# Values as the stationary operand in the second attention's two branches, with the probabilities scaled on VectorE before they are flipped

## What is computed

```
o_c = softmax(q kc^T) vc            # compressed keys, 31 of them
o_s = softmax(q ks^T, causal) vs    # selected blocks: with 512 tokens all of them are selected
o_w = softmax(q kw^T, causal) vw    # window of 512: the same reach
y_b = g_c * o_c + g_s * o_s + g_w * o_w
merged = gate_a * (y_a @ w_br_a) + gate_b * (y_b @ w_br_b)
```

## Time and profile before

| what | us |
|---|---|
| three runs, median (lowest to highest) | 1233.98 (1233.65 to 1234.14) |
| the profiled execution, its own time | 1236.62 |
| span of that execution, first to last instruction | 1234.8 |
| TensorE busy in it | 1197.2 (97%) |
| VectorE, GpSimd, ScalarE busy | 632.7, 676.4, 318.0 |
| the 64 steps, from the first score matmul to the last weigh matmul | 646.3 to 799.9 |
| first matmul on `yb_hi` | 803.9 |

### The profile page before, as it was taken

One profiled execution on the slowest core, in us unless ns is written; L12 is line 12 of the kernel. 1 busy time (PEld: TensorE's weight loads), 2 busy tenths in 40 slices (PEclk: granted clock), 3 DMA queues, 4 the chain that ended last, 5 costly groups with the idle time before them and its releaser, 6 DMA issues.

```text
span 1234.8 us, 18903 instructions
## 1 busy us (share of the span) xinstructions
PE 1197.2 (97%) x6856; PEld 985.0 (80%) x6856; DVE 632.7 (51%) x1212; ACT 318.0 (26%) x667; POOL 676.4 (55%) x610
## 2 busy tenths in 40 slices
PE   7999999998999999999999999999999999999997
PEld 6777778777987787877788888878888888888885
DVE  3885654478732576563876666572353300335022
ACT  3125112124632322211234454420221100113001
POOL 4884443343526587665743334356666666666662
PEclk9999999998799899999999999999999999999998
DMA  7221121114003222223531111122232332333321
GB/s 246 86 85 55 50 55 49 53 53 120 1 18 110 70 85 85 85 69 102 210 107 35 52 52 38 52 82 87 85 101 88 100 102 88 99 102 104 101 85 68
DMA packets 29684, 102.41 MB, mean 83 GB/s; under 512 B 3632, under 2 KB 6064, under 8 KB 28848
## 3 DMA queue, kind: packets, MB, share of 16 engines
q1 hardware_dynamic: 27232, 93.47, 24.1%
q10 hardware_dynamic: 2384, 7.99, 1.9%
HBM read 95.16 MB, written 2.10 MB: 79 GB/s over the span
## 4 chain that ended last, share of the span: by engine, by line
PE 85%; DVE 6%; POOL 4%; issue 2%; ACT 2%; DMA 1%; SPq 0%; DVEq 0%; POOLq 0%; ACTq 0%
PE acc L277 23%; PE acc L279 22%; PE acc L278 22%; POOL w_lo L1544 3%; PE aux L488 3%; PE aux L1600 2%; PE aux L478 2%; PE aux L344 1%; PE aux L1584 1%; PE aux L869 1%; PE acc L488 1%; PE aux L870 1%; DMA residual<-x 1%; PE aux L782 1%; DVE conv_sum L1911 1%
## 5 line engine op out<-in xcount | busy, mean ns | idle before, releaser
L1536 POOL CAST w_hi<-w_raw 128x1024 fp32r<-128x1024 f32 x164 | 177.7, 1083 | 504.2 <-issue 365.9
L1544 POOL TENSOR_TENSOR w_lo<-w_raw,w_hi 128x256 fp32r<-128x256 f32 x352 | 290.2, 855 | 7.0
L277 PE MATMUL acc<-ht_hi,w_hi 128*128 128x512 f32 x672 | 272.8, 406 | 6.3 <-DVE ht_lo L388 2.5
L279 PE MATMUL acc<-ht_hi,w_lo 128*128 128x512 f32 x672 | 264.2, 393 | 0.0
L278 PE MATMUL acc<-ht_lo,w_hi 128*128 128x512 f32 x672 | 263.7, 392 | 0.0
L1539 POOL TENSOR_TENSOR w_lo<-w_raw,w_hi 128x1024 fp32r<-128x1024 f32 x76 | 188.3, 2477 | 6.1
L277 PEld LDWEIGHTS acc<-ht_hi,w_hi 128*128 128x128 f32 x672 | 127.1, 189 | 37.2 <-POOL w_lo L1544 6.0
L279 PEld LDWEIGHTS acc<-ht_hi,w_lo 128*128 128x128 f32 x672 | 127.1, 189 | 27.6
L278 PEld LDWEIGHTS acc<-ht_lo,w_hi 128*128 128x128 f32 x672 | 127.4, 190 | 24.3 <-issue 1.2
L277 PE MATMUL acc<-w_hi,ht_hi 128*128 128x512 f32 x256 | 106.8, 417 | 0.3
L277 PE MATMUL acc<-w_hi,ff_hi 128*128 128x512 f32 x256 | 100.4, 392 | 2.3 <-POOL w_lo L1539 2.3
(11 more groups left out here) (413 smaller groups left out, 1949.4 us busy)
## 6 DMA issues: line engine op xcount, KB each, us to landing
w_raw<-units SPq DMA_DIRECT2D x164, 512.0 KB, 3.5
cmp_w<-w_kv ACTq DMA_DIRECT2D x4, 1024.0 KB, 7.8
residual<-x SPq DMA_DIRECT2D x4, 512.0 KB, 7.1
k_turned<-k_split SPq DMA_DIRECT2D x8, 256.0 KB, 5.0
result<-normalized SPq DMA_DIRECT2D x4, 512.0 KB, 2.6
consts_sb<-consts SPq DMA_DIRECT2D x1, 1120.5 KB, 7.3
k_turned<-k_split ACTq DMA_DIRECT2D x2, 512.0 KB, 5.9
norm_post_sb<-norm_post ACTq DMA_DIRECT2D x1, 512.0 KB, 4.2
```

The source lines that it names most:

```text
L277: nc.tensor.matmul(bank, ah, bh, start=start, stop=False)
L279: return nc.tensor.matmul(bank, al, bh, start=False, stop=stop)
L1536: nc.gpsimd.tensor_copy(w_hi[:, slot], raw[:, j]).then_inc(hi_split, 1)
L1544: done = nc.gpsimd.tensor_tensor(w_lo[:, slot, kk, cols], raw[:, j, kk, cols], w_hi[:, slot, kk, cols].bitcast(F32), ALU.subtract)
```

## The change

The values become the stationary operand (64 columns) and the flipped probabilities the moving one (128 columns). The two heads of a pair, both of one group, write to partitions 0 to 63 and 64 to 127 of the same bank, so that the result is features by tokens. The steps are reordered for that: n % 2 is the head of the pair, n % 8 // 2 the tile t. `weigh` runs once for a pair of steps, and in TensorE's order it stands ahead of `flip`. The reciprocal and the gate can no longer be applied to the result, where tokens lie along the columns; VectorE multiplies both onto the probabilities instead, between the exponential and the flip (`scale_probs`), and adds the result of a pair with `add_values`. `YB` becomes `YT`, features by tokens, so its flips at the end are gone, and the high and low parts of its chunks 0 to 2 are made within the steps. The compressed branch is written by feature too: 4 head pairs with 512 columns in place of 4 tiles with 2 x 256.

```diff
+            def flip(n):
+                branch, k, g, t, h = branch_step(n)
+                pe.wait_ge(values_used, SELECTED + n + 2)
+                if n:
+                    pe.wait_ge(probs_out, SELECTED + n)
+                for j in range(t + 1):
+                    done = nc.tensor.transpose(flips_to[:, j * P:(j + 1) * P], pr2[:, h, j * P:(j + 1) * P], ident)
+                done.then_inc(probs_flipped, 1)
+            def weigh(pair):
...
+                pe.wait_ge(probs_out, SELECTED + 2 * pair + 2)
+                pe.wait_ge(values_used, SELECTED + 2 * pair + 3)
...
+                for j in range(t + 1):
+                    for h in range(2):
+                        done = nc.tensor.matmul(values_to[h * DH:(h + 1) * DH, 0:P], VSW[:, j, a:a + DH],
+                                                pt2[:, h, j * P:(j + 1) * P], start=j == 0, stop=j == t)
+                done.then_inc(weighed, 1)
+            for n in range(BRANCH_STEPS):
+                scores(n + 1)
+                fill(n)
+                if n and n % 2 == 0:
+                    weigh(n // 2 - 1)
+                flip(n)
+            def scale_probs(n):
+                branch, k, g, t, h = branch_step(n)
+                w, m = (t + 1) * P, n % 16
+                eng.wait_ge(probs, SELECTED + n + 1)
+                step(nc.vector.reciprocal(rs8[:, m:m + 1], psum_[:, m:m + 1]))
+                nc.vector.tensor_scalar(pr2[:, h, :w], pr2[:, h, :w], rs8[:, m:m + 1], gate(branch, 2 * k + h, t),
+                                        ALU.mult, ALU.mult).then_inc(values_used, 1)
+            def add_values(pair):
+                y = YT[:, k, t * P:(t + 1) * P]
+                eng.wait_ge(weighed, SELECTED + pair + 1)
+                done = nc.vector.tensor_tensor(y, y, aux[3][:, 0:P], ALU.add)
+            for n in range(BRANCH_STEPS + 2):
+                if n < BRANCH_STEPS:
+                    negate(n)
+                    if 1 <= n % 8 < 5 and n < BRANCH_STEPS - 8:
+                        done = stage(n // 8 + 1, n % 8 - 1)
...
+                if 1 <= n <= BRANCH_STEPS:
+                    scale_probs(n - 1)
+                if n >= 3 and n % 2:
+                    add_values((n - 3) // 2)
+                beside(n)
...
+            def high_part(k):
+                act.wait_ge(on["y_summed"], k + 1)
+                nc.scalar.activation(yb_hi[:, k], YT[:, k], ACT.Copy).then_inc(flip_hi, 1)
...
+                if n in (46, 51, 59):
+                    high_part((n - 43) // 8 if n > 46 else 0)
...
-            for t in range(NT):
-                pe.wait_ge(on["c_flip_out"], t // 2 + 1)
+            pe.wait_ge(on["c_flip_out"], 2)
+            for k in range(4):
...
-            flip_on_tensor(pe, lambda t, k: YB[:, t, k * P:(k + 1) * P], 4, FLIP_B)
+            branches_on_tensor(pe, branch_fill)
```

## The result

| kernel | us, median (lowest to highest) | ratio to before | steps |
|---|---|---|---|
| before | 1233.83 (1233.65 to 1234.14), 4 runs | 1 | 153.8 |
| after | 1256.30 (1253.66 to 1258.51), 4 runs | 1.0174, 95% interval 1.0157 to 1.0191 | 178.6 |

The account below looks back on a forecast made before the run. TensorE was taken to bound the steps. -5.8 (weigh) + 27.5 (waits) - 4.0 (end) + 0.9 (compressed branch) = +18.6, with 1.4 for the clock +20: profiled 1236.6 becomes 1256.6, median 1254, range 1243 to 1270.

Parts of the forecast that it names:

- The weigh: TensorE's weigh matmuls in the steps: 25.1 us against 30.9, a gain of 5.8.
- whether the halves overlap: Weigh: rival that the two column halves don't overlap, 42.5 us in place of 25.1, time 1268; chance 0.05.
- The waits: TensorE's waits in the steps: 31.5 us with VectorE disturbed, 26.5 undisturbed; less 4 today, +27.5.
- the chain: Within a step: scores, negate, any stage, reciprocal, scaling on VectorE, then flip; fixed parts 0.74 us, covered by piece and weigh.
- The scaling's price: VectorE's scale_probs: 0.28, 0.35, 0.41, 0.48 us by width, taken from L1469.
- the rival built on it: Scaling at the price of L1190: 0.28 to 0.48 us more in waiting steps, time 1269; chance 0.06.
- The end: From the last weigh to the product on yb_hi: flips gone, early chunks already split, 4.0 us gained.
- The compressed branch: Its matmul waits for the second move; first score at 647.1, not 646.27: 0.9 us lost.
- The clock: Steps: a fall of the granted clock behind long waits; one costs at most 1.7 us, 1.4 added.
- the rival of some falls: Steps: waits bring on some falls of the clock, time 1261; chance 0.06.
- The rival of a clock that stays low: Steps: a stretch that stays at 1.2 GHz, time up to 1300; chance 0.03.
- The covered chain: Steps: VectorE's chain ends inside the piece, so only the savings are left, 1217; chance 0.07.

Follow-up runs that it names:

- e4: The changed kernel with the weigh's loops turned round, all key blocks for one head, then for the other: 1262.54 us, ratio to before 1.0230.
- e1: The changed kernel with scale_probs(n-1) put ahead of negate(n) and the staging of queries on VectorE: 1227.60 us, ratio to before 0.9948.
- e2: The changed kernel with only the staging of queries moved behind scale_probs(n-1), negate(n) still ahead: 1239.34 us, ratio to before 1.0043.
- e3: The changed kernel with scale_probs multiplying only the first column, the rest left unscaled: 1246.06 us, ratio to before 1.0096.
- e11: The changed kernel with the reciprocal of scale_probs made twice in each of 64 steps: 1264.35 us, ratio to before 1.0242.
- e5: The changed kernel with its nine steps without a piece moved to 2, 10, 18 to 58 and 63: 1257.41 us, ratio to before 1.0163.
- e7: The changed kernel with six useless 512-column matmuls added in each of the nine steps without a piece: 1258.47 us, ratio to before 1.0188.
- e6: e1 with the nine steps without a piece moved to 2, 10, 18 to 58 and 63: 1229.66 us, ratio to before 0.9954.
- e12: e1 with the reciprocal of scale_probs made twice in each step: 1233.85 us, ratio to before 0.9992.
- e8: e1 with the high and low parts of all four chunks of y_b put behind the 64 steps: 1233.40 us, ratio to before 0.9987.
- e10: e6 with step 6's output-gate piece made between the compressed branch's last matmul and the first score: 1229.67 us, ratio to before 0.9949.

## Why the prediction was right, step by step

**The weigh**, 25.1 us forecast. By the four widths measured (0.47, 0.69, 0.90 and 1.13 a pair with the way in) it is 25.5. The doubt whether the halves overlap as in the earlier trace rows is settled by these widths and by e4. The Trainium skill, "TensorEngine Tiling (Array Packing)", Performance Considerations, gives a factor of 2 for this swap, which would have made 15.5 us of it; the trace shows 25.5, since a pair of records takes 0.109 (12 records take 0.22 more than 8) and each of the 32 pairs pays about 0.25 for going in and out.

**The waits**, 31.5 us forecast. Flips lose 29.0 from start to start, and weighs that wait for L792 about 2: 31. Step by step the chain held:

| us lost at the flip | forecast, undisturbed | measured, mean |
|---|---|---|
| n % 8 = 1 | 0.41 | 0.57 (undisturbed 0.39) |
| 2 | 0.30 | 0.63 (undisturbed 0.39) |
| 3 | 0.90 | 1.01 |
| 5 | 0.37 | 0.42 |
| 7 | 0.04 | 0.03 |
| step 13, 27, 34, 41, 55 | 1.76, 2.29, 1.69, 1.80, 1.43 | 1.72, 2.31, 1.57, 1.79, 1.27 |
| step 6, 20, 48, 62 | 0.94, 0.95, 0.56, 0.94 | 0.70, 0.71, 0.07, 0.72 |

The means are those of the steps with a piece up to 55; a step right behind a long wait loses less. The even empty steps lose 1.2 us less in all than forecast. The disturbance of VectorE makes about what was set for it: undisturbed steps stand near the forecast, the means above them (ahead of the flip of step 26 a stage of 0.69 takes 0.96). One slip of the forecast, without weight: 1254 less the 5 us of disturbance is 1249, not 1248.5.

**The scaling's price**, the unknown of the forecast: 0.28 to 0.48, and 0.15 to hand over. Undisturbed it takes 0.35, 0.41, 0.48 and 0.55, and the flip starts 0.05 behind its end, where other waits had 0.15. The two errors cancel: 0.40 to 0.60 from its start to the flip's, against 0.43 to 0.63. The reading of L1190 in the earlier trace rows as disturbed fits the traces, and the rival built on it (1269) is out: in before all four L1190 run wholly beside a split of GpSimd (L1544; from 460.84 to 461.80 for the first, the splits from 460.46 to 463.10). In after 14 of the 64 scalings take over 5% longer than their width does undisturbed, up to 1141 ns, and each of them runs beside a split or a cast of GpSimd; none of the 45 without GpSimd beside them does. So the double duration occurs, but not as the rule. A run without GpSimd's splits was not made. The Trainium skill, "VectorE: DVE Perf Modes", The TRN2 errata, gives 58 + FD/Accel cycles, by which 512 columns would take an estimated 0.33 us; the trace has 0.55.

**The end**, 4.0 gained: 3.9. **The compressed branch**, 0.9 lost: from the start of the second move to the first score 4.26 before (642.01 to 646.27), 5.14 after:

```profile
643.51 0.60 ACT L1142 ACTIVATE cmp_probs_t<-aux 128x512 f32<-128x512 f32 x1 [1.22 <-PE aux L958]
644.16 3.80 PE L966 MATMUL aux<-cmp_probs_t,cmp_values 128*128 128x512 f32 x8 [0.69 <-ACT cmp_probs_t L1142]
...
648.65 0.33 PE L753 MATMUL aux<-k_split,q_split_even 128*128 128x128 f32 x1 [0.69 <-ACT y_b_by_feature L1146]
```

The other 1.5 us by which the first score is late arise ahead of the branch, where the change does nothing: they are the fall of the clock between 104 and 112 named above, which before's profiled execution does not have.

**The clock** was the term that was mis-sized: 1.4 us for one fall, and there were three, 5.1 us. By this the rival of some falls (1261, given 0.06) came true in kind, though the time stayed below its figure. In e1 the steps less their waits are 150.3 - 5.3 (flips) - 3 (weighs) = 142.0 us. For after, 142.0 + 29.0 + 2 leaves 5.6 of the 178.6, and three falls of 1.7 are 5.1. The same account closes within about 1 us for e2 (no fall), e3 (one), e11 (two), e4 (the worth of four, one fall being twice as long, and its 6 us of longer weighs) and e5 (five); e7 stands 3 to 4 us above it, with no fall, of which its groups of six, longer than 1.39, make 1. So a fall costs nearly its full 1.7 us, and the waits in it cover little. That the time still came out near is in part luck, an error the other way: the work in the steps was put at 143.9 (149.7 less the 5.8 of the weigh), 1.9 too high. Where these 1.9 lie is not settled.

The four runs of after lie from 1253.7 to 1258.5 with mean granted clocks of 0.986, 0.987, 0.980 and 0.982 in the order of their times. The four of before lie within 0.5, but a larger set does not: of the 26 runs of before beside e6 the fastest took 1228.95 at 0.991 and the slowest 1238.31 at 0.980. So the scatter goes with the clock in both kernels. Only a profiled execution shows where the clock falls, and whether the falls in the steps differ from run to run is not shown. The rival of a clock that stays low did not occur.

**The covered chain**, the faster rival at 1217, did not occur either, for the reason given: the order makes the chain. e1 is this rival with the order put right: 1227.6. It stays above 1217 since that was the bound without edges at the weigh, and since 8 us of waits are left.

## What to carry to other kernels

When an operation is moved from behind a product to ahead of it, ask first what stands in front of it in its engine's order, and whether any of that waits for something which the waiting engine issues late in the same step. Put what is waited for ahead of what only has to be done some time: here that was worth 28 us, where taking nearly the whole width out of the scaling (e3) was worth 10.7, both with the falls of the clock that went with it. Then try how much slack is left by adding a known operation to the chain, since a chain without visible waits can be tenths of a microsecond from waiting (e12).

## What the runs showed of the hardware

TensorE starts matmuls of the other column half ahead of earlier ones in the program. The records do not say which half they belong to, so this is worked out from times. In e4, with four records of one half written ahead of four of the other, the eight records start in pairs, as if the halves alternated, and take 0.67 (0.66 when they do). Less the 0.27 of one record, the starts spread over 0.40; at 0.109 for each, one half after the other, it would be 7 x 0.109 = 0.76. With six and six they take 1.14 against 0.88, with eight and eight 1.58 against 1.09. A reach of four records fits all three: two, or four, records at either end would then find no partner, which makes an estimated 0.22 and 0.44 us more; measured were 0.26 and 0.49. Only these widths were run. So the order in which TensorE's program is written is not in every case the order of its starts.

A VectorE operation shows a record that ends after the next one has begun: the scaling of 128 columns takes 0.35, and the next operation starts 0.26 behind its start (703.68 to 703.94 in e1). What waits for its result on TensorE starts 0.05 behind the record's end, what stands behind it on VectorE 0.09 ahead of it.

The falls of the clock came with long waits of TensorE. In the profiled executions the steps of e1, e6, e8 and e10 have one wait of over 1 us and no fall, e12 three (the longest 2.0), e2 four (2.2) and e7 four (1.4) and no fall; e3 has five and one fall; after has eight and three falls, e4 and e5 nine each and the worth of four and five; but e11 has 14 (the longest 2.4) and two. So neither the length nor the number of the waits sorts these kernels alone, and no run here separates the two.
